# A hybrid attention trunk on one core: attention steps of one chunk and key group, unpadded V in column tiles, and x released per k

## The reference

```python
def sink_attention(q, k, v, valid, sinks):
    s = jnp.einsum('bqngd,bknd->bngqk', q, k).astype(jnp.float32)
    s = jnp.where(valid, s, -jnp.inf)
    sk = sinks.astype(jnp.float32).reshape(1, ATT_KV_HEADS, ATT_GROUP, 1, 1)
    m = jnp.maximum(jnp.max(s, -1, keepdims=True), sk)
    e = jnp.exp(s - m)
    p = e / (jnp.sum(e, -1, keepdims=True) + jnp.exp(sk - m))
    return jnp.einsum('bngqk,bknd->bqngd', p.astype(v.dtype), v)
```

## Time and profile before

| | |
|---|---|
| median of 3 runs (lowest to highest) | 1546.15 us (1545.23 to 1547.86) |
| profiled execution, its own time | 1542.32 us |
| span of the profile, first to last instruction | 1540.6 us |
| PE busy | 1487.6 us (97%) |
| PE weight loads busy | 1442.7 us (94%) |
| DVE busy | 975.0 us (63%) |
| ACT busy | 563.4 us (37%) |
| POOL busy | 169.4 us (11%) |
| mean granted clock of TensorE | 0.984 |

### The profile page before, as it was taken

One profiled execution on the slowest core, in us unless ns is written; L12 is line 12 of the kernel. 1 busy time (PEld: TensorE's weight loads), 2 busy tenths in 40 slices (PEclk: granted clock), 3 DMA queues, 4 the chain that ended last, 5 costly groups with the idle time before them and its releaser, 6 DMA issues.

```text
span 1540.6 us, 26157 instructions
## 1 busy us (share of the span) xinstructions
PE 1487.6 (97%) x10213; PEld 1442.7 (94%) x10213; DVE 975.0 (63%) x1748; ACT 563.4 (37%) x989; POOL 169.4 (11%) x186
## 2 busy tenths in 40 slices
PE   7999998999999999999998989999999999999996
PEld 6988998999999999999998967899999999999996
DVE  4366676448666666676577378536766666666655
ACT  4145354434232323233343157524333332323222
POOL 1013220121000000000032000021000000000000
PEclk9999999999999999999999989999999999999999
DMA  6421333432222122112206300021222222212102
GB/s 227 128 83 57 112 102 101 136 110 83 82 82 82 54 82 82 58 51 81 83 1 142 116 28 1 13 83 55 84 81 82 82 82 82 82 64 72 54 1 93
DMA packets 104360, 122.17 MB, mean 79 GB/s; under 512 B 13315, under 2 KB 96201, under 8 KB 104025
## 3 DMA queue, kind: packets, MB, share of 16 engines
q1 hardware_dynamic: 104188, 121.27, 24.4%
q10 hardware_dynamic: 108, 0.03, 0.0%
HBM read 109.43 MB, written 11.95 MB: 79 GB/s over the span
## 4 chain that ended last, share of the span: by engine, by line
PE 91%; DVE 5%; ACT 2%; issue 1%; POOL 0%; DMA 0%; SPq 0%; DVEq 0%; ACTq 0%
PE ps L368 54%; PE ps L529 18%; PE ps L1764 7%; PE ps L1007 2%; DVE x_lo L440 1%; PE ps L547 1%; PE ps L992 1%; PE ps L379 1%; PE ps L393 1%; PE ps L1809 1%; PE ps L972 1%; PE ps L1822 1%; PE ps L1846 1%; PE ps L1842 0%; DVE x_res L493 0%
## 5 line engine op out<-in xcount | busy, mean ns | idle before, releaser
L368 PE MATMUL ps<-x_hi,w_hi 128*128 128x320 f32 x1888 | 431.3, 310 | 7.4 <-DVE x_lo L440 6.9
L368 PE MATMUL ps<-x_lo,w_hi 128*128 128x320 f32 x1888 | 430.2, 309 | 0.0
L368 PE MATMUL ps<-x_hi,w_lo 128*128 128x320 f32 x1888 | 430.2, 309 | 0.0
L368 PEld LDWEIGHTS ps<-x_hi,w_hi 128*128 128x128 f32 x1888 | 315.4, 188 | 9.4 <-issue 4.7
L368 PEld LDWEIGHTS ps<-x_hi,w_lo 128*128 128x128 f32 x1888 | 315.7, 188 | 0.0
L368 PEld LDWEIGHTS ps<-x_lo,w_hi 128*128 128x128 f32 x1888 | 315.6, 188 | 0.0
L348 ACT ACTIVATE w_hi<-w_raw 128x1024 fp32r<-128x1024 f32 x138 | 145.0, 1060 | 423.4 <-PE ps L368 382.2
L493 DVE TENSOR_TENSOR x_res<-x_res,ps 128x640 f32<-128x640 f32 x192 | 153.7, 817 | 130.1 <-PE ps L368 66.1
L355 DVE TENSOR_TENSOR w_lo<-w_raw,w_hi 128x1024 fp32r<-128x1024 f32 x138 | 169.7, 1236 | 33.6 <-ACT w_hi L348 26.4
L611 DVE TENSOR_TENSOR up_rows<-ps,rstd_cols 128x320 f32<-128x320 f32 x88 | 43.1, 490 | 164.6 <-PE ps L368 164.6
L529 PE MATMUL ps<-gated_hi,d_hi 128*128 128x320 f32 x640 | 145.8, 309 | 0.0
(11 more groups left out here) (269 smaller groups left out, 1901.3 us busy)
## 6 DMA issues: line engine op xcount, KB each, us to landing
w_raw<-in_ffn_w_up_dram SPq DMA_DIRECT2D x44, 1024.0 KB, 5.2
d_raw<-in_ffn_w_down_dram SPq DMA_DIRECT2D x22, 1024.0 KB, 5.0
w_raw<-in_gla_w_in_dram SPq DMA_DIRECT2D x12, 1024.0 KB, 6.1
seq_states<-in_state_gla_dram SPq DMA_DIRECT2D x4, 1024.0 KB, 5.5
out_dram<-seq_states SPq DMA_DIRECT2D x4, 1024.0 KB, 8.3
w_raw<-in_gla_w_out_dram SPq DMA_DIRECT2D x4, 1024.0 KB, 5.3
w_raw<-in_att_w_q_dram SPq DMA_DIRECT2D x4, 1024.0 KB, 6.8
w_raw<-in_att_w_o_dram SPq DMA_DIRECT2D x4, 1024.0 KB, 5.0
```

Of the source, the lines that this page charges most:

```text
L368: mm = pe.matmul(PS[:, 2 * (u0 % 4) + f, 0:HALF], w[:, n0 % 4, k, :], x[:, k, f * HALF:(f + 1) * HALF], start=(k == 0 and a == 0), stop=(k ...
```

## The change

The attention steps become (chunk, key group): 8 heads, four blocks of 128 rows. There are 16 for the prompt and 4 for the sample (two sequences each). V is kept once, without zeros (`VP`, `VS`), and a block of 64 output rows is a column tile of PE; the own-chunk part of two blocks is transposed together (64 keys of each) and multiplied in 64 by 64 tiles. Queries of the sample go into `QS` by POOL, without zeros. The transposed probabilities are in two banks, one for the 128-key part (`PTA`, copied by ACT) and one for the own part (`PTB`, copied by DVE). Scores of step 0 are computed ahead of query tile 7. The first half of a second output tile is computed before the last outputs are ready. In the two last output tiles before an up projection, a semaphore `x_free` counts the k that are done, and ACT and DVE convert x of that k.

```diff
-        NATT = (TT - 1) * KT + NS
+        ATT_STEPS = [(0, 0), (1, 0), (0, 1), (1, 1)] + [(c, g) for c in range(2, SEQ // CH) for g in range(KVH)]
+        NPR = len(ATT_STEPS)
+        NATT = NPR + NS // 2
...
-            if beside is not None:
-                mm = beside()
+                if release and k < KT - 1:
+                    mm.then_inc(x_free, 1)
...
-            for j in range(KT):
+            for j in range(KT - 1):
                 add_x(v, j, u0 + j)
-                if j < KT - 1:
-                    rest_tile(v, n0 + 4 + j)
-            for k in range(KT):
-                if k == 2:
-                    rest_tile(v, n0 + 4 + KT - 1)
+                rest_tile(v, n0 + 4 + j)
+            for k in range(KT - 1):
                 rest_x(v, k, vec, base)
+            add_x(v, KT - 1, u0 + KT - 1)
+            rest_x(v, KT - 1, vec, base)
+            rest_tile(v, n0 + 4 + KT - 1)
...
-            act.wait_ge(full, u0 + KT)
-            for k in range(KT):
-                if k == 2:
-                    round_tile(act, n0 + 4 + KT - 1)
-                if k == 4:
-                    act.wait_ge(free, u0 + KT)
-                    square_x(act, KT - 1, norm)
-                if k == KT - 1:
-                    act.wait_ge(free, u0 + KT)
+            for k in range(KT - 1):
+                act.wait_ge(x_free, (KT - 1) * (n0 // T_AO) + k + 1)
                 round_x(act, k, vec)
+            act.wait_ge(free, u0 + KT)
+            round_x(act, KT - 1, vec)
+            square_x(act, KT - 1, norm)
+            round_tile(act, n0 + 4 + KT - 1)
...
+            sp.dma_start(VS[0:CH, :], VP[CH:128, :]).then_inc(s_vs, 16)
+            sp.dma_start(VS[CH:128, 0:TT - 2], VP[0:CH, 1:TT - 1]).then_inc(s_vs, 16)
+            sp.dma_start(VS[CH:128, TT - 2], VP[0:CH, 0]).then_inc(s_vs, 16)
+            sp.dma_start(VC[:, :, :, :].rearrange("p s g d -> p s (g d)"),
+                         A["cache_v"].rearrange("s k g d -> k s (g d)")).then_inc(s_vn, 16)
...
+            for j in range(KT):
+                pool.wait_ge(free, u_q(j) + 1)
+                for c in range(2):
+                    mm = pool.tensor_tensor(QS[:, 4 * c:4 * c + 4, j // 4, SL * (j % 4):SL * (j % 4) + SL],
+                                            QF[:, j // 2, SEQ // CH + c, j % 2, :].rearrange("p (s t) -> p s t", t=SL),
+                                            ones[:, 0:CH].rearrange("p (s t) -> p s t", t=SL), ALU.mult)
+                mm.then_inc(qz, 1)
...
+                if n < NPR:
+                    c, g = ATT_STEPS[n]
                     k0, nk = window(c)
+                    for y in range(2):
+                        for a in range(2):
+                            h = slice(HD * a, HD * a + HD)
+                            mm = pe.matmul(PS[:, score_bank(n) + a, nk * y:nk * y + nk],
+                                           QF[h, 2 * g + y, c, :, :].rearrange("p m q -> p (m q)"),
+                                           KTD[h, g, k0:k0 + nk], start=True, stop=True, tile_position=(HD * a, 0))
                 else:
+                    for x in range(2):
+                        s_ = 2 * (n - NPR) + x
+                        if s_ == 0:
+                            pe.wait_ge(qz, KT)
+                        for g in range(KVH):
+                            for e in range(2):
+                                h = slice(HD * e, HD * e + HD)
+                                mm = pe.matmul(PS[h, score_bank(n) + x, (WIN + SL) * g:(WIN + SL) * (g + 1)],
+                                               QS[h, s_, g, :], KCT[h, g, s_, :],
+                                               start=True, stop=True, tile_position=(HD * e, HD * e))
...
+                if n:
+                    pe.wait_ge(a_pt, n)
+                    if both(n - 1):
+                        pe.wait_ge(a_ptb, both(n - 1))
+                if n >= NPR:
+                    for j in range(4):
+                        for x, k in enumerate((WIN, SL)):
+                            mm = pe.transpose(PS[0:k, prob_bank(x), 128 * j:128 * j + 128],
+                                              probs(n, WIN * x + (WIN + SL) * j, k), ident[:, :])
+                else:
+                    w = keys_of(n)
+                    w0, w1 = key_parts(n)
+                    for j in range(4 if w0 else 0):
+                        mm = pe.transpose(PS[:, prob_bank(0), 128 * j:128 * j + 128],
+                                          probs(n, w * j + (CH * (j % 2) if w1 else 0), 128), ident[:, :])
+                    for y in range(2 if w1 else 0):
+                        mm = pe.transpose(PS[:, prob_bank(1), 128 * y:128 * y + 128],
+                                          probs(n, 2 * w * y + (128 if w0 else 0), 128), ident[:, :])
...
+                b, o = n % 2, out_bank(n)
+                if n == 0:
+                    pe.wait_ge(s_vs, 16 * 3)
+                if n >= NPR:
+                    if n == NPR:
+                        pe.wait_ge(s_vn, 16 * (NS + 1))
+                    for j in range(4):
+                        s_, g = 2 * (n - NPR) + j // 2, j % 2
+                        for e in range(2):
+                            c = slice(128 * j + HD * e, 128 * j + HD * e + HD)
+                            pe.matmul(PS[HD * e:HD * e + HD, o, HD * j:HD * j + HD], VC[:, s_, g, :], PTA[:, b, c],
+                                      start=True, stop=False, tile_position=(0, HD * e))
+                        for e in range(2):
+                            c = slice(128 * j + HD * e, 128 * j + HD * e + HD)
+                            mm = pe.matmul(PS[HD * e:HD * e + HD, o, HD * j:HD * j + HD], VN[:, s_, g, :],
+                                           PTB[0:SL, b, c], start=False, stop=True, tile_position=(0, HD * e))
                 else:
+                    c, g = ATT_STEPS[n]
+                    w0, w1 = key_parts(n)
+                    if w0:
+                        for a in range(2):
+                            vv, t = v_rows(c - 2 + a if w1 else 0, 0)
+                            mm = pe.matmul(PS[HD * a:HD * a + HD, o, 0:256], vv[:, t, g, :],
+                                           PTA[:, b, :].rearrange("p (y a q) -> p y a q", y=2, a=2)[:, :, a, :],
+                                           start=True, stop=not w1, tile_position=(0, HD * a))
+                    if w1:
+                        for a in range(2):
+                            h = slice(HD * a, HD * a + HD)
+                            vv, t = v_rows(c - 2 * a if w0 else c, a)
+                            mm = pe.matmul(PS[h, o, 0:256], vv[h, t, g, :], PTB[h, b, 0:256],
+                                           start=not w0, stop=True, tile_position=(HD * a, HD * a))
...
+            for j in range(4, 8):
+                fm_tile(pe, T_AQ + j, u_q(j))
+                if j == 6:
+                    scores(0)
+            for n in range(1, NATT + 3):
                 if n < NATT:
                     scores(n)
                 if n == NATT + 1:
                     pe.wait_ge(lo_done, T_AO + 1)
                     pe.wait_ge(a_ex, NATT - 1)
+                    pe.wait_ge(a_ol, 2 * HALF // CH)
                     fm_half(pe, T_AO, U_AO, 0)
                 if 2 <= n < NATT + 2:
                     transposes(n - 2)
                 if n >= 3:
                     values(n - 3)
+            pe.wait_ge(lo_done, T_AO + 2)
+            pe.wait_ge(a_ex, NATT)
+            fm_half(pe, T_AO + 1, U_AO + 1, 0)
             pe.wait_ge(a_ol, NATT)
+            for j in range(2):
+                fm_half(pe, T_AO + j, U_AO + j, 1).then_inc(full, 1)
+            for j in range(2, KT):
+                fm_tile(pe, T_AO + j, U_AO + j, release=j == KT - 1)
...
+        def prob_bank(part):
+            return 2 * ((U_AO + 2) % 4) + part
...
+            def maxima(n):
+                v.wait_ge(a_sc, n + 1)
+                b = n % 2
+                w = keys_of(n)
+                sc = PS[:, score_bank(n):score_bank(n) + 2, 0:2 * w].rearrange("p a (y k) -> p a y k", y=2)
+                if n < NPR:
+                    g = ATT_STEPS[n][1]
+                    m = NM[:, b, :].rearrange("p (y a) -> p a y", a=2)
+                    o, sink, se = NM[:, b, :], SKP[:, 4 * g:4 * g + 4], SE[:, b, :]
+                else:
+                    m = NM[:, b, :].rearrange("p (s g) -> p s g", s=2)
+                    o, sink = m, SKR[:, :].rearrange("p (s g) -> p s g", s=1).to_broadcast([128, 2, KVH])
+                    se = SE[:, b, :].rearrange("p (s g) -> p s g", s=2)
+                v.tensor_reduce(m, sc, AX.X, ALU.max).then_inc(a_chain, 1)
+                v.wait_ge(a_chain, 2 * n + 1)
+                v.tensor_tensor(o, o, sink, ALU.max).then_inc(a_chain, 1)
+                v.wait_ge(a_chain, 2 * n + 2)
+                v.tensor_tensor(se, sink, o, ALU.subtract)
+                v.tensor_scalar(NM[:, b, :], NM[:, b, :], -1.0, None, ALU.mult).then_inc(a_nm, 1)
```

(98 more changed lines are left out.)

153 lines of the change are left out of this document (25 added, 128 removed).

## The result

The new kernel takes 1501.08 us (median of 4 runs, 1498.96 to 1503.71) against 1545.75 before (also 4 runs): ratio 0.9709, 95% interval 0.9689 to 0.9729. The direction was forecast; 1501 lies under the range of 1505 to 1533. Its profiled execution took 1503.71 (span 1501.8), 38.6 less than the one of before, where the sum said 29.3.

What follows compares the result with a forecast made beforehand. PE was taken to bound the kernel (91% of the span). Terms -16.5 - 3.1 - 4.5 + 0.6 + 0 - 5.8 = -29.3 took 1542.3 to 1513.0, plus 3.8 for the median: 1517 us, range 1505 to 1533.

Steps and rivals of the forecast that it cites:

- Sample steps: Attention stage: 8 sample steps become 4, PE sets the pace at 4.4 us each, 17.6 against 20.7: -3.1 us.
- The end: From the last scores to the output projection's second tile: 19.5 us before and after, so 0; bounds -3 and +1.
- The start: Last query tile to first three-chunk reduction: DVE's queue gives -7.9, a low PE clock takes +3.4; -4.5 us.
- Three-chunk steps: Attention prompt steps with three chunks, 24 become 12: DVE sets the pace at 3.4 us each; -16.5 us.
- x per k: Two places where ACT and DVE convert x while the last output tile runs: 2 x -2.9 = -5.8 us.
- Rival 5: DVE is quicker than its sum, PE's 2.9 sets the pace: -6 to -9, 1509 us; chance 0.08.
- Rival 4: Converting x during the last output tile gains nothing because DVE comes too late: 1523 us; chance 0.05.
- Rival 3: Own-chunk products and sample scores: row halves sharing a bank run one after the other; +6, 1523 us; chance 0.13.
- The rule on changes of arrangement: PE's value products: each change of row count costs 0.1 us extra, adding 0.2 us a sample step.
- Rivals 1 and 2: Attention stage, PE at 1.2 GHz: half of it, +17, 1534, chance 0.15; all the way, 1561 us, chance 0.04.
- The basis: Profiled execution's 1542.3 less the sum gives 1513.0; the median of the runs stands 3.8 above it: 1517 us.

## Why the prediction was wrong, step by step

The mechanisms were mostly right, but a piece of work was counted twice. Between the two profiled executions the saving was 9.3 us larger than the sum: the terms missed 11.35, and 2.0 were lost outside the changed places. The step from these executions to the medians took the rest.

- **Sample steps (-3.1; measured -9.06): the step that failed most.** "PE sets the pace: 4.4. 4 x 4.4 = 17.6" put each sample step's value products into the step that carries its scores. They run three steps later (`values(n - 3)` in the diff): the steps with sample scores still multiply prompt values, and stand 3.03 apart. PE was full there, as forecast (9.04 of 9.10), but with less work. All four sample steps' values lie in the drain, where "two steps 6.7" and "two values 4.8" had counted them already. So I counted them twice: 3 x (4.4 - 3.03) = 4.1 of the miss of 6.0. The rest, 1.8, is the fourth step, which I counted as an interval although "The end" begins at its scores. The doubled products show it: nothing in the reductions, everything in the drain. The pieces were near: scores 0.98 (I had 1.1), transposes 1.02 (0.9), values 2.10 (2.4).
- **The start (-4.5; measured -8.26).** The -7.9 for DVE's queue was right. The step "so I let the clock fall again: for two of the new steps PE at 1.2 GHz, +3.4" failed: the clock did fall to 1.2 GHz, at 893.7, but was back at 900.5, with the first three-chunk step, and under DVE's queue it cost 0.39. The earlier scores, which I had as part of the gain, give 1.16 here and cost 0.80 in the query tiles. What is left goes with the number of small steps, as far as I can tell: four reductions stand ahead of the first three-chunk one where eight stood; that was not tried by itself.
- **Three-chunk steps (-16.5; measured -18.80).** DVE sets the pace, as forecast, at 3.27 instead of 3.4; the copy takes 0.33 start to start and the other pieces are a little shorter, 12 x 0.13 = 1.6. The first two steps, 2.69 and 2.95 apart, give the other 0.9. PE's 2.84 to 2.9 is 2.88 in the trace. Rival 5 (PE sets the pace) is excluded by the doubled transposes and the doubled copy.
- **End (0; measured +0.77).** Right within its bounds, but by luck. The 19.5 that I took from the kernel before held two half tiles slowed by the low clock (5.19 and 5.32), and I put the new ones in at full clock (3.5 each). The new kernel then lost 1.54 to the low clock as well, and its transposes and values took 6.25 and 4.20 where I had 6.7 and 4.8.
- **x per k (-5.8; measured -6.10)**, shown from both sides. Rival 4 is out.
- **Rival 3 (halves that share a bank run one after the other)** is out: the two own-chunk products, in different row halves and one bank, start together at 922.31 and take 0.43 each, and the four records take 0.58 on the chain, like the four of L1041 before them; 16 sample score records take 0.98, where I had 1.1 with two at a time. The Trainium skill (TensorEngine Tiling (Array Packing), Gotcha 1) says that different row tiles cannot access one PSUM bank at the same time; for tiles that write different partitions of the bank, as here, the trace differs, and the trace decides.
- **The rule on changes of arrangement.** The grouped products make 6 changes fewer a step and take 0.87 less, 0.15 each if all of it goes with the changes. The Trainium skill (TensorEngine Tiling (Array Packing), Key Properties) says that a change of mode drains the engine; the trace agrees. I used this rule as a reason against the sample part, and not as what it was: an order to improve.
- **Rivals 1 and 2 (the clock in the middle)** didn't come: 0.98 over the three-chunk steps. A low clock did come behind the sample values, where no rival had it, though the kernel before has one in the same place (0.91 from 963 to 1003 in the earlier trace rows).
- **The basis.** 1513.0 was for an execution like the profiled one, and I added 3.8 because the median of before stood that much above it. After, the first median stands 2.6 under its profiled execution: 6.4 of the 15.9 us between 1517 and 1501.1. All 14 runs of the new kernel have a median of 1502.4, and the later medians of the kernel before are 1544.3 to 1544.7, so part of this was chance.

## What to carry to other kernels

In a software pipeline, write down for each step which iteration of every operation it holds: a term for "a step with its values" is counted twice when the values lag into the drain. Where the engines of a step are close (here DVE, PE and ACT busy 36.70, 33.13 and 31.59 of 38.36 us), look for a copy that the least loaded one can take; here 0.33 us moved from DVE to ACT shortened the step by all of it, and left the three about level. Order small products so that products with the same arrangement stand together.

## What the runs showed of the hardware

A PE that the profile shows busy without a pause does not by itself keep the clock: alternating groups of four 64-column records, 128 and 16 rows, were followed by 1.2 GHz (0.94 granted over 27.27 us, 0.73 over 43.84 us when issued twice), while the same records grouped by kind kept 2.4 GHz (1.00), twice as many included. The kernel before, whose sample products alternate too, had 0.87 in that stretch. What in the alternation brings it was not tried.
